# Encoder kernel: first tokens normalised in halves, lower halves of the last projection last, and GpSimd instead of VectorE weighing the first half's rows

## The reference

```
layer 0: h = rms_norm(x, pool_norm)
         u, gate = h @ w_in (1024 -> 2048 + 2048)
         diff = centred_window_mean(u, window 2, 4, 8, 16 by feature group) - u
         x = x + ((diff @ w_group, per group) * scale * silu(gate)) @ w_out
layer 1: h = rms_norm(x, att_norm)
         q, k, v for 3 dilation groups of 8 heads of 128, and a gate: h @ w_in (1024 -> 10240)
         o_g, lse_g = windowed attention with dilation 1, 4, 16 (g = 0, 1, 2)
         o = sum over g of softmax_g(lse_g) * o_g
         x = x + (o * silu(gate)) @ w_out
```

## Time and profile before

| | |
|---|---|
| median of 3 runs | 1664.0 us |
| the profiled execution's own time | 1664.83 us |
| its span, first to last instruction | 1663.0 us |
| PE busy | 1650.5 us (99%), 8288 matmuls |
| DVE busy | 1139.6 us (69%) |
| ACT busy | 840.4 us (51%) |
| POOL busy | 271.0 us (16%) |
| granted TensorE clock | 1.00 in every stretch |

### The profile page before, as it was taken

One profiled execution on the slowest core, in us unless ns is written; L12 is line 12 of the kernel. 1 busy time (PEld: TensorE's weight loads), 2 busy tenths in 40 slices (PEclk: granted clock), 3 DMA queues, 4 the chain that ended last, 5 costly groups with the idle time before them and its releaser, 6 DMA issues.

```text
span 1663.0 us, 23746 instructions
## 1 busy us (share of the span) xinstructions
PE 1650.5 (99%) x8288; PEld 1402.0 (84%) x8288; DVE 1139.6 (69%) x1896; ACT 840.4 (51%) x1980; POOL 271.0 (16%) x292
## 2 busy tenths in 40 slices
PE   8999999999999999999999999999999999999999
PEld 7888888888888888888888888888888889999887
DVE  6886677787976697686868357875368346666565
ACT  6453333432431463475655245564456257886463
POOL 1000000004312110141423012230014000005440
PEclk9999999999999999999999999999999999999999
DMA  5133333484511424332332415242324656767784
GB/s 180 52 130 124 121 108 102 152 324 157 177 46 56 148 102 150 104 121 83 127 114 89 137 66 171 82 134 96 127 78 153 229 169 227 246 221 237 241 299 159
DMA packets 146134, 242.60 MB, mean 146 GB/s; under 512 B 17249, under 2 KB 55137, under 8 KB 144994
## 3 DMA queue, kind: packets, MB, share of 16 engines
q1 hardware_dynamic: 141122, 223.79, 40.2%
q10 hardware_dynamic: 4896, 17.30, 2.8%
HBM read 161.23 MB, written 79.82 MB: 145 GB/s over the span
## 4 chain that ended last, share of the span: by engine, by line
PE 81%; ACT 1%; DVE 0%; DMA 0%; issue 0%; ACTq 0%; DVEq 0%
PE pair L1215 23%; PE pair L1217 23%; PE pair L1216 23%; PE pair L1567 4%; PE pair L1539 3%; PE pair L1487 3%; PE pair L1547 2%; ACT pp L2695 1%; DMA raw<-in_pool_w_in_dram 0%; PE pair L1236 0%; ACT turn L2746 0%; ACT qT L2688 0%; DVE w L1729 0%; ACT turn L2761 0%; DVE both L2294 0%
## 5 line engine op out<-in xcount | busy, mean ns | idle before, releaser
L1215 PE MATMUL pair<-w,turnh 128*128 128x512 f32 x640 | 249.0, 389 | 0.0
L1216 PE MATMUL pair<-w,turnh 128*128 128x512 f32 x640 | 249.0, 389 | 0.0
L1217 PE MATMUL pair<-w,turnl 128*128 128x512 f32 x640 | 249.0, 389 | 0.0
L1215 PE MATMUL pair<-w,hTh 128*128 128x512 f32 x544 | 214.0, 393 | 0.0
L1217 PE MATMUL pair<-w,hTl 128*128 128x512 f32 x544 | 212.0, 390 | 0.0
L1216 PE MATMUL pair<-w,hTh 128*128 128x512 f32 x544 | 211.7, 389 | 0.0
L2663 ACT ACTIVATE both<-pair 128x512 f32<-128x512 f32 x160 | 94.0, 591 | 176.4 <-PE pair L1217 167.6
L2157 DVE TENSOR_TENSOR both<-pair,both 128x512 f32<-128x512 f32 x120 | 81.5, 687 | 111.8 <-PE pair L1217 111.4
L2674 ACT ACTIVATE dump<-both 128x128 f32<-128x128 f32 x384 | 119.4, 311 | 64.0 <-DVE both L2157 51.5
L1215 PEld LDWEIGHTS pair<-w,turnh 128*128 128x128 f32 x640 | 120.1, 188 | 25.1 <-DVE turnl L1786 0.2
L1217 PEld LDWEIGHTS pair<-w,turnl 128*128 128x128 f32 x640 | 120.1, 188 | 25.0
(11 more groups left out here) (248 smaller groups left out, 3813.1 us busy)
## 6 DMA issues: line engine op xcount, KB each, us to landing
part_spill<-both SPq DMA_DIRECT2D x160, 256.0 KB, 3.7
both<-part_spill SPq DMA_DIRECT2D x22, 1024.0 KB, 7.2
raw_z<-in_att_w_in_dram SPq DMA_DIRECT2D x20, 1024.0 KB, 5.3
raw<-in_pool_w_in_dram SPq DMA_DIRECT2D x32, 512.0 KB, 5.2
raw<-in_att_w_in_dram SPq DMA_DIRECT2D x10, 1024.0 KB, 6.1
raw_u<-in_att_w_in_dram SPq DMA_DIRECT2D x10, 1024.0 KB, 5.7
diff_spill<-ubuf SPq DMA_DIRECT2D x16, 512.0 KB, 2.7
stage<-gate_spill SPq DMA_DIRECT2D x16, 512.0 KB, 5.8
```

The lines of the kernel that those rows point to most:

```text
L1215: nc.tensor.matmul(out, lh, rh, start=first, stop=False, skip_group_check=onto)
L1216: nc.tensor.matmul(out, lh, rl, start=False, stop=False, skip_group_check=onto)
L1217: return nc.tensor.matmul(out, ll, rh, start=False, stop=last, skip_group_check=onto)
```

## The change

1. *Start.* The two passes for each half of the weight row signal separately. Blocks 0 and 1 are both scaled, transposed and cut in halves of 512 features (`scale_half`, `lows_half`), and so is the first weight unit's low part (`split_half`). PE runs the first quarter of unit 0 in three rounds (`first_quarter`): all high times high, then low weight times high, then high times low rows. ACT's `square(2)` moves ahead of the copy of the weight row; the waits on the transposes' results are changed to fit. The warm-up matmuls between the transposes go.
2. *Pairs of layer 0.* `add_quarter(n, 2)` moves behind the low parts of products 5 and 6.
3. *Attention.* ACT's `take_u` moves from h = 0 to h = 1, and from step 35 on to h = 2. `SPREAD` moves from h = 0 to h = 2 of the same steps.
4. *Merging.* For rows 0 to 7 POOL, not DVE, multiplies `u` by its factors.
5. *Last projection.* `project_out` issues the eight matmuls with the high part of y, then waits for its low part, then issues the other four. The last half row is computed, added and stored in two parts of 256 features.

```diff
-        SPREAD = {(42, 0): (6, 0), (43, 0): (6, 1), (44, 0): (7, 0), (45, 0): (7, 1)}
+        SPREAD = {(42, 2): (6, 0), (43, 2): (6, 1), (44, 2): (7, 0), (45, 2): (7, 1)}
...
-                for hf in range(2):
-                    sp.wait_ge(out_added, 2 * m + hf + 1)
-                    sp.dma_start(dst[:, hf, :], xb[m % 4][:, hf, :]).then_inc(out_sent[m % 4], 16)
+                for i, (hf, at) in enumerate(((0, slice(0, 512)), (1, slice(0, 256)), (1, slice(256, 512)))):
+                    sp.wait_ge(out_added, 2 * m + i + 1)
+                    sp.dma_start(dst[:, hf, at], xb[m % 4][:, hf, at]).then_inc(out_sent[m % 4], 16)
...
 (gpsimd, merge_rows)
+                if m < TB:
+                    pool.wait_ge(uin[u_place(m)[0]], 16 * 3 * u_place(m)[1])
+                    u4 = u.rearrange("p g (h e) -> p g h e", h=HALF)
+                    nc.gpsimd.tensor_tensor(u4, u4, fac[:, 0:2, b, :].unsqueeze(3).to_broadcast([P, 2, HALF, HD]),
+                                            ALU.mult).then_inc(u_weighed, 1)
...
 (tensor, start)
+            def first_quarter():
...
+                for kd in range(KD):
+                    pe.wait_ge(half_then_row_kept if kd < HB else hhi_done, 2)
+                    nc.tensor.matmul(out, wh[:, kd, :], rowsh[:, kd, quarter], start=(kd == 0), stop=False)
+                for kd in range(KD):
+                    pe.wait_ge(*((dve_step, 5) if kd < HB else lo_ready(0)))
+                    nc.tensor.matmul(out, wl[:, kd, :], rowsh[:, kd, quarter], start=False, stop=False)
+                for kd in range(KD):
+                    pe.wait_ge(hlo_half if kd < HB else hlo_done, 2)
+                    nc.tensor.matmul(out, wh[:, kd, :], rowsl[:, kd, quarter], start=False, stop=(kd == KD - 1))
...
-            warm_up(3)
-            transpose_x(0, 0)
-            warm_up(3)
-            transpose_x(0, 1)
+            for part in range(2):
+                for tb in range(2):
+                    pe.wait_ge(*((dve_step, tb + 3) if part == 0 else (xn_done, tb + 1)))
+                    for kd in range(HB * part, HB * part + HB):
+                        last = nc.tensor.transpose(x_pair(0, tb)[:, kd * P:kd * P + P],
+                                                   (bufU, bufS)[tb][:, kd * P:kd * P + P], ident[:, :])
+                    last.then_inc(xt_done if part else row_spread_then_half, 1)
...
 (tensor, project_out)
-                    pe.wait_ge(ylo_done, m + 1)
+                    pe.wait_ge(yhi_done, m + 1)
...
+                if (m, hf) == (NROW - 1, 1):
+                    for part in range(2):
...
+                        last.then_inc(zo_done, 1)
+                    return
                 for j in range(HALF):
-                    last = three(...)
+                    for lo in (False, True):
+                        nc.tensor.matmul(out_bank(m, hf), y_turned(m % 2, False)[:, j, :],
+                                         out_w(2 * (m // TB * HALF + j) + hf, lo), start=(j == 0 and not lo), stop=False)
+                if hf == 0:
+                    pe.wait_ge(ylo_done, m + 1)
+                for j in range(HALF):
+                    last = nc.tensor.matmul(out_bank(m, hf), y_turned(m % 2, True)[:, j, :],
+                                            out_w(2 * (m // TB * HALF + j) + hf, False), start=False,
+                                            stop=(j == HALF - 1))
...
 (vector, norm_x(0))
-                    scale(0)
-                    scale(1)
-                    split_lo(0)
-                    lows(0)
-                    lows(1)
+                    scale_half(0, 0).then_inc(dve_step, 1)
+                    scale_half(1, 0).then_inc(dve_step, 1)
+                    split_half(0).then_inc(dve_step, 1)
+                    steps[0] += 3
+                    scale_half(0, 1).then_inc(xn_done, 1)
+                    scale_half(1, 1).then_inc(xn_done, 1)
+                    lows_half(0, 0)
+                    lows_half(1, 0)
+                    split_half(1).then_inc(w_lo, 1)
+                    lows_half(0, 1)
+                    lows_half(1, 1)
                     scale(2)
...
 (vector, pairs of layer 0)
                     split_product(n + 1, 4)
-                    add_quarter(n, 2)
                     split_product(n + 1, 5)
                     split_product(n + 1, 6)
+                    add_quarter(n, 2)
...
 (vector, merge)
-                    if part == 0:
+                    if part == 0 and m >= TB:
...
 (scalar, norm_x(0))
+                    square(2)
                     act.wait_ge(xn_done, 2)
                     nc.scalar.activation(bufG[:, :], pair[1][:, :], ACT.Copy).then_inc(half_then_row_kept, 1)
-                    square(2)
...
 (scalar, attention)
-                if h == 0 and 2 <= t <= NSTEP + 1:
+                if h == (1 if t <= merge_step(0) else 2) and 2 <= t <= NSTEP + 1:
                     take_u(t - 2)
```

More of the change, by code:

```diff
@@ L1264, in _ @@
             for hf in range(2):
-                last = nc.tensor.matmul(pair[1][:, 512 * hf:512 * hf + 512], bufU[:, 0:P], bufS[:, 512 * hf:512 * hf + 512],
-                                        start=True, stop=True)
-            last.then_inc(row_spread_then_half, 1)
-            warm_up(3)
-            transpose_x(0, 0)
-            warm_up(3)
-            transpose_x(0, 1)
+                nc.tensor.matmul(pair[1][:, 512 * hf:512 * hf + 512], whole[:, 0, 0:P], bufG[:, 512 * hf:512 * hf + 512],
+                                 start=True, stop=True).then_inc(row_spread_then_half, 1)
+            for part in range(2):
[5 more added lines that the diff above has]
+                    last.then_inc(xt_done if part else row_spread_then_half, 1)
             warm_up(4)
@@ L1276, in _ @@
                     if c == 0 and q == 0:
-                        pe.wait_ge(hlo_done, 1)
-                        pe.wait_ge(hlo_half, 1)
+                        first_quarter()
+                        transpose_x(0, 2)
+                        continue
                     elif c == 0:
@@ L1281, in _ @@
                     elif c == 1 and q == 0:
-                        pe.wait_ge(half_then_row_kept, 2)
+                        pe.wait_ge(half_then_row_kept, 3)
                     if q == 0:
@@ L1791, in lows @@
                     n = layer * TB + tb
-                    if n == 1:
-                        for part, (high, low) in enumerate(((half_then_row_kept, hlo_half), (hhi_done, hlo_done))):
-                            kds = slice(KD // 2 * part, KD // 2 * (part + 1))
-                            dve.wait_ge(high, 1 if part == 0 else 2)
-                            nc.vector.tensor_tensor(rowsl[:, kds, P:2 * P],
-                                                    x_pair(0, 1)[:, 512 * part:512 * part + 512].rearrange(
-                                                        "p (k c) -> p k c", c=P),
-                                                    rowsh[:, kds, P:2 * P].bitcast(F32), ALU.subtract).then_inc(low, 1)
-                        return
                     if layer:
@@ L2293, in add_rows @@
                 part = xb[m % 4][:, hf, :]
+                if (m, hf) == (NROW - 1, 1):
+                    for i in range(2):
+                        at = slice(256 * i, 256 * i + 256)
+                        dve.wait_ge(zo_done, 2 * m + 2 + i)
+                        nc.vector.tensor_tensor(part[:, at], bank(5 + i)[:, at], part[:, at],
+                                                ALU.add).then_inc(out_added, 1)
+                    return
                 nc.vector.tensor_tensor(part, out_bank(m, hf), part, ALU.add).then_inc(out_added, 1)
@@ L2394, in highs @@
                     n = layer * TB + tb
-                    if n == 1:
-                        for part, (turned, high) in enumerate(((row_spread_then_half, half_then_row_kept), (xt_done, hhi_done))):
-                            kds = slice(KD // 2 * part, KD // 2 * (part + 1))
-                            act.wait_ge(turned, 2)
-                            nc.scalar.activation(rowsh[:, kds, P:2 * P],
-                                                 x_pair(0, 1)[:, 512 * part:512 * part + 512].rearrange(
-                                                     "p (k c) -> p k c", c=P), ACT.Copy).then_inc(high, 1)
-                        return
                     act.wait_ge(xt_done, n + 1)
```

63 lines of the change are left out of this document (45 added, 18 removed).

## The result

The changed kernel took 1673.47 us (median of 5 executions, 1672.30 to 1674.65); the kernel before, beside it on the same chip, took 1664.48 us (5 executions, 1662.98 to 1665.48). The ratio is 1.0053, 95% interval 1.0039 to 1.0067: 9.0 us slower, where 4.65 us faster was forecast. The profiled execution took 1674.65 us itself; its span is 1672.6 us against 1663.0.

A forecast was written before the change was run, and what follows sets the result against it. PE was taken as the bound, so only its stalls could be won: 2.5 + 0.3 + 0.45 + 1.1 + 0 + 0.3 = 4.65 us, giving 1659.4 us against the median of 1664.0; 8-in-10 range 1657.2 to 1662.0.

The forecast's parts named there:

- ACT's copy: Attention: moving ACT's copy of the values gains 0.45 us at step 31, elsewhere nothing, or costs up to 0.3 once.
- The half about step 32: Attention: with the copy gone from between, PE's next transpose starts at about 1499.55 instead of 1500.00, 0.45 us gained.
- SPREAD: Steps 42 to 45: projections at h = 2 cut PE's stalls from 2.64 to 1.55 us, gain 1.1.
- The start: First units: unit 1's first matmul at 16.95 instead of 19.50 us, gain 2.5 us, bounds 1.9 and 2.9.
- the end: Last projection: last half row in two parts, net 0.3 us gained, bounds 0 and 0.6.
- GpSimd at zero: Rows 0 to 7 of merging: the multiplication moved from DVE to GpSimd gains nothing, upper price 0.5 us at row 1.
- rival C: Merging: GpSimd's multiplication makes its row exceed the 10.8 us pitch and holds PE; 1672 us at 7.5 us each; 5%.
- The pairs: Layer 0: a 1.1 us load stall goes, two of about 0.37 and 0.43 come; 0.3 us gained.
- Rival A: Gains given back: start limited to 1.9 us, steps 42 to 45 gain 0, pairs -0.2; 1661.8 us; 23%.
- My 6% for slower: Chance given to a slower kernel: rival C and a little for what had not been seen, 0.06.

The follow-up runs named there:

- e9: Kernel before with one instruction moved, ACT's copy of the values at step 41 from h = 0 to h = 2; 1671.39 us against 1664.26.
- e1: Changed kernel with ACT copying the values at h = 0 again from step 35 on; 1666.84 us against 1663.69 for the kernel before.
- e4: Kernel before with only ACT's value copies moved, to h = 1 up to step 34 and h = 2 behind it; 1669.75 us against 1663.69.
- e7: e1 with ACT's high parts of the last output weight's two halves one and two heads later; 1662.27 us against 1663.97 for the kernel before.
- e8: e7 with the loads of x blocks 4 and 5 also issued later, as in e5; 1660.76 us against 1663.97 for the kernel before.
- e12: e8 with the projections of rows 6 and 7 back at h = 0; 1662.50 us against 1664.26 for the kernel before.
- e5: Kernel before with the new start, and loads of x blocks 4 and 5 issued behind ACT's high part of block 2; 1662.19 us against 1663.97.
- e10: Kernel before with the projections' low halves last and the last half row in two parts; 1663.56 us against 1664.26.
- e11: Kernel before with add_quarter(n, 2) alone moved behind the low parts 5 and 6; 1664.97 us against 1664.26.
- e6: Kernel before with only the projections of rows 6 and 7 moved from h = 0 to h = 2; 1667.35 us against 1663.97.
- e2: Changed kernel with the projections of rows 6 and 7 back at h = 0; 1670.60 us against 1663.69 for the kernel before.
- e3: Changed kernel with VectorE again multiplying the first half's rows instead of GpSimd; 1671.91 us against 1663.69 for the kernel before.
- e13: e8 with VectorE again multiplying the first half's rows instead of GpSimd; 1660.71 us against 1663.82 for the kernel before.

## Why the prediction was wrong

**The step that failed** is the sentence on ACT's copy: "Elsewhere the copy moves to a place where ACT has room, behind a projection of 2.8 us on PE: nothing. If it has no room there, it costs up to 0.3 us once." It asked whether ACT had room for the instruction, and not who waits for what the instruction makes. SP does, and SP's list is in order: the store of step 41 came 5.7 us later (4.7 in e9, where nothing ahead of it has moved), and with it the loads of rows 8 and 9 and both output weights behind it. In place of nothing, or 0.3 us, this one copy cost 7.1 us (e9); the return of all copies from step 35 on gave back 5.8 of the 9.0 us (e1). The half about step 32 was nearly right: that stall of 0.45 is gone, but one of 0.18 us came 2.3 us ahead of it, and in e4 0.36 us are gained.

**SPREAD** failed in a second way. The sum of small stalls was good (1.55 forecast, 1.65 in e7 and e8), if partly by luck, and so was the gain in clean surroundings (1.1 forecast, 1.0 in e12 against e8 without the longer last wait). What it left out was a resource with no slack: it followed ACT's list by durations and took each output weight as landed. The trace of before had the warning, ACT's wait of 0.96 us for the last one at 1595.79, hidden only because a projection covered it; in e5, e10 and e11, where nothing of these steps was changed, the same landing cost PE 1.16, 1.09 and 1.24 us by itself. e6: 4.11 us of stall for this part alone.

**The start**: 2.5 us were forecast, with the sentence "Behind it the quarters repeat with the same distances between PE, ACT and DVE, so the gain stays." Unit 1 did come 2.0 us earlier, at 17.46 (16.95 forecast), but the earlier `square(2)` also issues block 4's load earlier, at 12.32, and so ahead of the load of unit 2's weights at 13.29; before, it came behind it (13.51 after 13.02). The prediction moved the square and not the load that it issues. Unit 2's weights then took 7.2 us to land in place of 4.9. Block 5's load moved too, from 3.1 us behind these weights' to 0.7 behind. Counted from PE's first instruction, block 4 came 0.5 us earlier in e1, e2 and e3 than in the trace of before, and 0.2 earlier than in the median of the six old starts, in place of 2.5. e5 shows the cause: with both loads behind, it is 2.67 us against the trace of before, and 2.0 from median to median of all traces of each kind. In the profiled execution of the changed kernel the clock also went down behind the stall, which cost 1.7 us more; the traces of e1, e2, e3 and e7 have the stall (1.8 us) without the dip.

**The rest**: the end right (0.3 forecast, 0.5 by e10's trace, 0.4 by the changed kernel's). GpSimd at zero right (e13), and rival C with it wrong; the slower outcome came by another way. The pairs were right in what happened and wrong in price: a stall seen once was taken for one that is always there. (The first new stall comes out at 0.31 us from the prediction's own numbers, 281.69 - 281.38, not 0.37; 0.31 was measured.)

Rival A had named landings "close to their use" for the start only, and as a limit on the gain, not as a loss. My 6% for slower held no case in which a transfer becomes later than before.

## What to carry to other kernels

Before an instruction is moved, follow its result and not its engine: through each semaphore to the queue that waits on it, and down that in-order queue to everything behind. Where DMA share was near 1.0 here, a late issue wasn't made good (e9: store 4.7 us late, last weight 5.4) and an early one gained little (e6: 2.2 us earlier, 0.2 gained). Every wait on a landing in the trace of before, even a covered one of under 1 us, says that the slack is zero: put it against each cover that the change takes away, and look in several traces how long it gets. A stall that one trace shows may be there in a third of executions only; look for it in several before pricing its removal.

## What the runs showed of the hardware

PE's granted clock went to 0.50 (1.2 GHz) in or behind long stalls and stayed there for a while though PE had work again. In the changed kernel it is 0.50 over 1602 to 1606, while the stall of 7.7 us ends at 1604.38, and 1.00 again over 1608 to 1610. In e9 it is 0.50 over 1604 to 1606, behind a stall of 3.88 us that ends at 1602.08; in e6 over 1596 to 1600, around the end of one of 4.11 us at 1596.35. In the changed kernel a wait of 2.04 us at the start was followed by it too, while four other kernels (e1, e2, e3, e7) with 1.75 to 1.84 us there kept 1.00 to 30 us. In the changed kernel each of the two stalls so cost 1.6 to 1.7 us beyond its own length; with what margin it is spared isn't shown by these runs.

The last output weight, 512 KB, took 8.9 to 13.3 us from issue to ACT's use in the 16 traces, wherever it was issued, against a median of 4.6 us from issue to landing over all eight such loads of the changed kernel. The 8.9 is the trace of before; no other has less than 10.5.

GpSimd and VectorE held each other up. In the kernel before, two of L1198's twelve multiplications took 2.02 and 2.03 us in place of 1.04, both started 0.4 us behind VectorE's weighing (L2264, two inputs in SBUF), which itself took 1.50 and 1.53 us in place of 1.22. In e13 two took 2.02 and 2.03 us again, both begun beside the same operation; in the changed kernel, where GpSimd has the weighing, the longest is 1.05.
